# VectorE's order in an RWKV-7 mixer, state banks taken in two pairs, and a transpose step in two parts

## The chip, the core and the metric

The kernel runs on one core of one Trainium2 chip. The metric is the device time of one execution in microseconds (us), the median of several runs. A core has TensorE (matrix products and transposes, PE in the rows; its weight loads are PEld), VectorE (DVE), ScalarE (ACT), GpSimd (POOL) and SyncE (SP), which issues most of the DMAs. The engines run their own instruction streams and meet only at semaphores.

## The reference, cut to what matters

A trunk of two layers on x (512 tokens, 1024 features) in float32. Layer 0, the one that the change touches, runs two head groups behind one input projection:

```python
p = h @ ev_w_in                                   # 512 x (1792 + 1024)
y_a = rwkv7_time_mix(p[..., :1792], ...)          # 8 heads of 64
y_b = rglru_block(p[..., 1792:2304], p[..., 2304:], ...)
h = LayerNorm(alpha * h + concat(y_a, y_b) @ ev_w_out)
# inside rwkv7_time_mix
kk = kk / max(norm(kk), 1e-12)                    # norms per head
state = state * w_t + (state @ -kk_t) (kk_t * a_t)^T + v_t k_t^T
o = state @ r_t                                   # for each of 512 tokens
o = (o - mean) * rsqrt(var + 64e-5) * gn_g + gn_b # "group" norm per head
y_a = (o + bonus) * g
# inside rglru_block
h_t = a_t * h_{t-1} + u_t;  y_b = h * gelu(gb)
```

Then follow cross-attention to 256 memory tokens and an MLP of width 4096, and layer 1 (a conformer convolution and Mamba-2) with its own attention and MLP. All that is outside the mixer of layer 0 is left as it was.

## The kernel before

Every product of activations and weights is made of float32r parts: ScalarE rounds a tensor to its high part (`w_hi`, `act_hi`), VectorE subtracts to get the low part (`w_lo`, `act_lo`), and TensorE multiplies hi*hi, lo*hi and hi*lo. The weights come in chunks of 128x1024 through three raw slots `w_raw`; SP refills a raw slot once VectorE's `split` has made the chunk's low part (`w_split`).

The order of each engine is written out by hand, as Python code that issues one instruction after the other. No planner moves anything. What is planned is the eight PSUM banks: the table `TILES` deals them out in turn, and `take(name, i)` on TensorE waits until the bank's former owner has been read.

The mixer of layer 0 handles its 8 heads in two blocks `b` of 4 heads (two 128-feature halves `j` each) and its 512 tokens in 8 chunks of 64. In order of TensorE:

- the input projection, 22 tiles (`feature_major`, L778), with small steps of block b between: `norms(b)` sums squares of kk into one bank, VectorE's `norm_scales(b)` makes 1/norm (L2199, L2200, signal `r_norm`), and `norms_back(b)` (L932) spreads it over the features again. In block 1 VectorE's loop step i == 17 ran two convolutions (`convolution`, L2234 and L2154) before `norm_scales(1)`.
- `within_chunks(b)`: 8 banks `rprod` of products between tokens of a chunk (L958), which VectorE multiplies by masks (`masked_products(b)`, eight instructions of L2151 that read a bank and `m_two`). In the same banks follow 8 tiles `rtok`, transposes to token rows: six of L968, two of L970 that also take a mean away. Each waits for the mask product of its own bank. ScalarE copies the `rtok` tiles out. Then the two gate products of the LRU (`lru`, L1146), for which VectorE makes `convolution(0..3)`.
- a solve by doubling, five levels for both blocks (L997, L1012; VectorE's `level_y` and `level_z`), started from `first_level(b)` on VectorE (three kinds of L2151 and a transpose, L2304, signal `r_x0`); then `solved`, `even_output` and `transitions(b)` (L1042), whose sums VectorE adds (`added(b)`, signal `rat_out`).
- `scan()`: the 7 chunk states are gathered in the four `rst` banks, two chunks to a half bank; `states_from_tokens` (L1073) fills them in four steps m of two chunks, and m = 0, 1 write `rst` 0 and 1, m = 2, 3 write `rst` 2 and 3. The `rst` banks are those of `rat` of block 0. The outputs go to four `ro` banks (L1091, L1111).
- the output projection `out0` (L852) starts with the LRU half of the features (k = 0 to 3). Between k = 2 and k = 3 it calls `even_back` (L1138): 16 transposes of the normed RWKV outputs `oall`, 4 feature tiles jj times 4 token tiles m. `group_variance(m)` and `group_scale(m)` on VectorE make `oall[:, m]` (two signals `ro_out` each). VectorE's `lru_lo(k)` makes the low part of LRU feature tile k (signal `mix_lo`, k + 1); after that a chain of five instructions for each of the last four tiles gives `mix_lo` 5 to 8.

SP's queue around this place: chunk 5 of `out0`, the load of `h`, chunk 6 of `out0` (which waits for the low part of chunk 3, made by VectorE's `split(FIRST["out0"] + 1 + W_SLOTS)`), the load of `gb` (which waits for `mix_done`), chunk 7.

GpSimd works beside it: `r_times_k(1)` (L638, a product of two tensors), and memsets `clear` (L642), of which the first two wait for the 22nd projection tile.

Of the kernel before, what the change touches and what calls it, by code (L numbers as in the profile page):

```python
# [20 lines left out]
P = 128  # L21
# [3 lines left out]
NT = T // P  # L25
# [203 lines left out]
def build(nc, x_tok, x_feat, mem_feat, weights, vectors, lora, lru_w, ln_rows, out):  # L229
    with ExitStack() as ctx:  # L230
# [523 lines left out]
        def _(pe):  # L754
            def take(stg, i):

                if AFTER[stg, i]:
                    pe.wait_ge(*out_sem(*AFTER[stg, i]))
                return bank(stg, i)
# [287 lines left out]
            def scan():  # L1047
# [10 lines left out]

                def states_from_tokens():

                    for i in range(4):
                        take("rst", i)
                    for m in range(NT):
                        for jj in range(4):
                            b, j = divmod(jj, 2)
                            kt, v_ = operands(b)[5:7]
                            for n, (lhs, rhs) in enumerate([(kt, v_), (NBT[b], NBH[b])]):
                                for q in range(2):
                                    feat, ct = slice(RD * q, RD * q + RD), cols_(2 * m, q)
                                    for c in (2 * m, 2 * m + 1):  # L1070
                                        if c < NRC - 1:
                                            tok = rows_(c)
                                            last = pe.matmul(state(c)[feat, jj * RD:jj * RD + RD], lhs[tok, j, ct],  # L1073
                                                             rhs[tok, j, ct], start=(m % 2 == 0 and jj == 0 and n == 0),
                                                             stop=False, skip_group_check=True)
                    last.then_inc(S("rst_mm"), 1)
# [54 lines left out]

            def even_back():

                pe.wait_ge(S("ro_out"), 2 * NT)
                for jj in range(4):
                    o = take("rback", jj)
                    for m in range(NT):
                        last = pe.transpose(o[:, m * P:m * P + P], oall[:, m, jj * P:jj * P + P], ident[:])  # L1138
                    last.then_inc(S("mixer_mm"), 1)

            def lru():
# [968 lines left out]
        def _(dve):  # L2110
# [131 lines left out]
            for i in range(22):  # L2242
                stg, n = PLACE0[i]
                tile = ORDER0[i]
                split(i + W_SLOTS)
                if i < 14:

                    dve.wait_ge(S("r_in"), i + 1)
                    cur = p0[:, tile, PAD + 1:PW]
                    done(stt(cur, bank(stg, n)[:, 0:T - 1], V("mu", tile), cur, MUL, ADD), "in_out")  # L2250
                if i == 5:
                    scaled_keys(0)

                    dve.wait_ge(S("masks"), 1)
                    step(dve.tensor_scalar(small[:, 84:88], vec[:, VEC["ka"]:VEC["ka"] + 4], -1.0, 1.0, MUL, ADD))
                if i == 6:
                    running_decay(0)
                    keys(0)
                if i == 9:
                    norm_scales(0)  # L2260
                if i == 11:
                    normalised(0)
                    scaled_keys(1)
                if i == 12:
                    scale_operands(0, 0)
                if i == 13:
                    scale_operands(0, 1)
                if i == 14:
                    bonus(0)
                if i == 16:  # L2270
                    running_decay(1)
                    keys(1)
                if i == 17:
                    for j in range(2):
                        dve.wait_ge(S("in_out"), 15 + j)
                        convolution(j)
                if i == 17:
                    norm_scales(1)
                if i == 19:
                    normalised(1)  # L2280
                if i == 20:
                    scale_operands(1, 0)
                if i == 21:
                    scale_operands(1, 1)
# [23 lines left out]
            convolution(2)  # L2308
            first_level(0, 0, 1)
            bonus(1)  # L2310
            first_level(0, 1, 2)
            masked_products(1)
            dve.wait_ge(S("in_out"), 18)
            convolution(3)
            first_level(1, 0, 2)
# [56 lines left out]
            lru_scan(0)  # L2372
            lru_scan(1)
            added(0)
            lru_scan(2)
            added(1)
            lru_scan(3)

            def lru_lo(k):
# [24 lines left out]
            lru_lo(1)  # L2404
            for m in range(2):
                group_scale(m)
            lru_lo(2)
            for m in range(2, 4):
                group_variance(m)
            lru_lo(3)  # L2410
            for m in range(2, 4):
                group_scale(m)
            split(FIRST["out0"] + 1 + W_SLOTS)
            for jj in range(4):
                y_ = p0[:, jj, PAD:PW]
                dve.wait_ge(*made("rback", jj + 1))
# [8 lines left out]
                    done(tt(act_lo[:, 3 + jj], p0[:, jj - 1, PAD:PW], f(act_hi[:, 3 + jj]), SUB), "mix_lo")  # L2425
            dve.wait_ge(S("mix_hi"), 8)
            done(tt(act_lo[:, 7], p0[:, 3, PAD:PW], f(act_hi[:, 7]), SUB), "mix_lo")
            done(dve.tensor_copy(small[:, 255:256], small[:, 254:255]), "mix_done")

            n_rows = [0]  # L2430
# [558 lines left out]
```

## Time and profile before

| what | value |
|---|---|
| median of 3 runs (lowest, highest) | 1607.37 us (1607.27, 1607.51) |
| the profiled execution's own time | 1606.2 us |
| its span (first to last instruction) | 1604.1 us |
| mean granted TensorE clock | 0.996 of full speed |
| busy: PE, PEld, DVE, ACT, POOL | 97%, 81%, 73%, 53%, 12% |
| instructions | 24420 |

The span is 2.1 us shorter than the execution's own time, and the profiled execution was 1.2 us faster than the median of the unprofiled runs. The mixer of layer 0 takes the span's first 259 us. TensorE is busy nearly everywhere, so the short idle times in front of its instructions, and the stretches where its instructions follow each other more slowly than elsewhere, are the places to look at.

### The profile page before, as it was taken

How to read it: one execution, taken by the hardware profiler on the slowest of the kernel's cores; microseconds unless marked ns; L12 is line 12 of the kernel's file. 1: busy time of each engine (PE TensorE's matmuls, PEld its weight loads, DVE VectorE, ACT ScalarE, POOL GpSimd, SP SyncE). 2: the span in 40 equal slices, each digit the busy share in tenths (PEclk: the TensorE clock that was granted, in tenths of full speed). 3: DMA queues.
4: the chain of work that ended last, by engine and by line, in shares of the span. 5: the costliest groups of instructions: out<-in, count | busy, mean ns of one | idle time of the engine just before them, and what ended most of it. 6: DMA issues, size and time to landing. Idle time of an engine off the chain costs nothing.

```text
span 1604.1 us, 24420 instructions
## 1 busy us (share of the span) xinstructions
PE 1563.4 (97%) x9706; PEld 1300.4 (81%) x9706; DVE 1177.2 (73%) x1356; ACT 843.6 (53%) x1087; POOL 193.6 (12%) x189
## 2 busy tenths in 40 slices
PE   9999999999999999999899999999999999999996
PEld 8777887988878788888778877889888788888885
DVE  4569767664778868686979986786557788676768
ACT  4645644464355454554468866635552654545454
POOL 6111201001100000000016743200020000000001
PEclk9999999999999999999999999999999999999999
DMA  6222004442151505151032330344411605050501
GB/s 215 79 79 67 16 4 151 145 151 68 53 216 47 182 28 172 39 171 40 14 136 77 104 92 14 132 158 133 157 54 56 241 20 195 29 171 26 195 1 53
DMA packets 40784, 159.57 MB, mean 99 GB/s; under 512 B 4064, under 2 KB 4192, under 8 KB 39264
## 3 DMA queue, kind: packets, MB, share of 16 engines
q1 hardware_dynamic: 40384, 155.93, 28.8%
q10 hardware_dynamic: 288, 2.10, 0.3%
q8 instruction: 77, 1.26, 0.3%
q14 instruction: 35, 0.29, 0.1%
HBM read 153.81 MB, written 4.19 MB: 99 GB/s over the span
## 4 chain that ended last, share of the span: by engine, by line
PE 80%; DVE 11%; ACT 5%; issue 2%; POOL 1%; ACTq 0%; DVEq 0%; POOLq 0%
PE bank L778 40%; PE bank L1457 15%; PE bank L852 14%; DVE h L2151 2%; POOL cacc L702 1%; PE bank L1012 1%; PE bank L997 1%; DVE h L2154 1%; DVE mix L2151 1%; ACT cprod L1944 1%; DVE a_lo L2151 1%; DVE lnst L2651 1%; PE bank L1367 1%; ACT sconv L1958 1%; DVE w_lo L2138 1%
## 5 line engine op out<-in xcount | busy, mean ns | idle before, releaser
L778 PE MATMUL bank<-act_hi,w_hi 128*128 128x512 f32 x840 | 330.7, 394 | 2.1 <-DVE sconv L2154 1.8
L778 PE MATMUL bank<-act_lo,w_hi 128*128 128x512 f32 x840 | 326.5, 390 | 0.0
L2138 DVE TENSOR_TENSOR w_lo<-w_raw,w_hi 128x1024 fp32r<-128x1024 f32 x173 | 219.3, 1272 | 133.1 <-ACT w_hi L1574 130.0
L1574 ACT ACTIVATE w_hi<-w_raw 128x1024 fp32r<-128x1024 f32 x173 | 183.0, 1061 | 111.1 <-PE bank L852 78.3
L778 PE MATMUL bank<-act_hi,w_lo 128*128 128x512 f32 x840 | 212.0, 390 | 0.0
L778 PEld LDWEIGHTS bank<-act_hi,w_hi 128*128 128x128 f32 x840 | 158.0, 188 | 38.4 <-issue 2.6
L778 PEld LDWEIGHTS bank<-act_lo,w_hi 128*128 128x128 f32 x840 | 157.8, 188 | 34.0 <-issue 1.2
L778 PEld LDWEIGHTS bank<-act_hi,w_lo 128*128 128x128 f32 x840 | 157.7, 188 | 32.9 <-DVE w_lo L2138 0.3
L702 POOL TENSOR_TENSOR cacc<-cacc,cprod 128x512 f32<-128x512 f32 x52 | 72.3, 1391 | 456.0 <-ACT cprod L1944 453.5
L1898 ACT ACTIVATE bank<-bank 128x512 f32<-128x512 f32 x64 | 37.2, 582 | 166.7 <-PE bank L778 166.7
L852 PE MATMUL bank<-w_hi,act_hi 128*128 128x512 f32 x288 | 112.6, 391 | 1.5 <-DVE act_lo L2151 1.5
L852 PE MATMUL bank<-w_hi,act_lo 128*128 128x512 f32 x288 | 112.1, 389 | 0.0
L1889 ACT ACTIVATE a_hi<-a_raw 128x1024 fp32r<-128x1024 f32 x48 | 51.0, 1062 | 67.9 <-PE bank L1457 62.8
L778 PE MATMUL bank<-act_hi,x_hi 128*128 128x512 f32 x208 | 81.5, 392 | 0.7 <-ACT act_hi L1801 0.6
L778 PE MATMUL bank<-act_lo,x_hi 128*128 128x512 f32 x208 | 80.9, 390 | 0.2
L1457 PE MATMUL bank<-w_hi,a_lo 128*128 128x512 f32 x264 | 73.0, 391 | 3.0 <-DVE a_lo L2151 3.0
L852 PE MATMUL bank<-w_lo,act_hi 128*128 128x512 f32 x288 | 74.7, 389 | 0.0
L1457 PE MATMUL bank<-w_hi,a_hi 128*128 128x512 f32 x264 | 72.5, 389 | 0.0
L1457 PE MATMUL bank<-w_lo,a_hi 128*128 128x512 f32 x264 | 71.3, 389 | 0.0
L2151 DVE TENSOR_TENSOR h<-h,bank 128x512 f32<-128x512 f32 x96 | 65.7, 684 | 2.0
L2138 DVE TENSOR_TENSOR w_lo<-b_raw,w_hi 128x1024 fp32r<-128x1024 f32 x46 | 55.4, 1223 | 15.8 <-ACT w_hi L1574 15.1
L852 PEld LDWEIGHTS bank<-w_hi,act_hi 128*128 128x128 f32 x288 | 54.0, 188 | 12.9 <-issue 1.6
(374 smaller groups left out, 3039.9 us busy)
## 6 DMA issues: line engine op xcount, KB each, us to landing
w_raw<-weights SPq DMA_DIRECT2D x199, 512.0 KB, 3.5
b_raw<-weights SPq DMA_DIRECT2D x32, 1024.0 KB, 4.9
gb<-ln_rows SPq DMA_DIRECT2D x6, 1024.0 KB, 9.8
stage<-x_feat SPq DMA_DIRECT2D x4, 512.0 KB, 6.1
h<-x_tok SPq DMA_DIRECT2D x1, 2048.0 KB, 8.0
stage<-mem_feat ACTq DMA_DIRECT2D x2, 1024.0 KB, 7.4
spill<-h SPq DMA_DIRECT2D x1, 2048.0 KB, 9.0
h<-spill SPq DMA_DIRECT2D x1, 2048.0 KB, 7.7
```

The costliest lines, as they stand in the source:

```text
L702: pool.tensor_tensor(cacc2[:, j % 2], cacc2[:, j % 2], cprod[:, added % 2], ALU.add)\
L778: return pe.matmul(banks[i][:, 0:n], w(c0 + i)[:, k * P:k * P + P], x[:, k, 0:n], start=first, stop=last)
L852: return pe.matmul(o[t][:, 0:HALF], x[:, slot[k], t * P:t * P + P], w(c0 + k // 2)[:, kk * HALF:kk * HALF + HALF], start=first, stop=last)
L997: last = each(lambda c, q, tok, feat, cf, ct: pe.matmul(compact(o, j, c, q, n), M_[b][tok, j, ct], halves(NBH[b][tok, j, ct], n, True), st ...
L1012: last = each(lambda c, q, tok, feat, cf, ct: pe.matmul(compact(o, j, c, q, n), left[tok, j, ct], halves(right[tok, j, ct], n, v < 5), sta ...
L1367: ins = pe.transpose(o[:, t * P:t * P + P], h[:, t, k * P:k * P + P], ident[:])
L1457: return pe.matmul(o[t][:], a[:, slot, k, t * P:t * P + P], w(c0 + k // 2)[:, k % 2 * HALF:k % 2 * HALF + HALF], start=(after is None and ...
L1574: act.activation(hi_slot(c), raw_chunk(c), ACT.Copy).then_inc(S("w_hi_done"), 1)
L1889: done(act.activation(a_hi[:, n % 2], A_OPERAND[name], ACT.Copy), "x_hi")
L1898: step(act.activation(o[:], o[:], ACT.Relu))
L2138: dve.tensor_tensor(lo_slot(c), raw_chunk(c), f(hi_slot(c)), ALU.subtract).then_inc(S("w_split"), 1)
L2151: return dve.tensor_tensor(o, a, b_, op)
```

## The change

No instruction that computes is added or taken away. Seven things move:

1. `norm_scales(1)` runs ahead of `convolution(0)` and `convolution(1)`.
2. `masked_products(1)` runs ahead of `first_level(0, 1, 2)`, the second half of block 0's first level with its transpose.
3. `added(1)` runs ahead of `lru_scan(2)`.
4. TensorE takes `rst` 0 and 1 before m = 0 and `rst` 2 and 3 before m = 2, instead of all four at the start.
5. `even_back` makes the tiles jj = 0 and 1 side by side, token tile by token tile, and waits for 4, 6 and 8 signals `ro_out`; jj = 2 and 3 follow whole. Before, it waited for all 8 first.
6. `lru_lo(2)` goes between `group_variance(2)` and `group_variance(3)`, and `lru_lo(3)` behind the last `group_scale`.
7. the low part of chunk 3 of `out0` is made behind the chain of the last four feature tiles instead of ahead of it.

```diff
 def states_from_tokens():
-    for i in range(4):
-        take("rst", i)
     for m in range(NT):
+        if m % 2 == 0:
+            for q in range(2):
+                take("rst", m + q)
...
 def even_back():
-    pe.wait_ge(S("ro_out"), 2 * NT)
-    for jj in range(4):
+    def turned(o, jj, m):
+        return pe.transpose(o[:, m * P:m * P + P], oall[:, m, jj * P:jj * P + P], ident[:])
+    pe.wait_ge(S("ro_out"), 4)
+    first = [take("rback", jj) for jj in range(2)]
+    for m in range(NT):
+        if m >= 2:
+            pe.wait_ge(S("ro_out"), 2 * m + 2)
+        for jj in range(2):
+            last = turned(first[jj], jj, m)
+            if m == NT - 1:
+                last.then_inc(S("mixer_mm"), 1)
+    for jj in range(2, 4):
         o = take("rback", jj)
         for m in range(NT):
-            last = pe.transpose(...)
+            last = turned(o, jj, m)
         last.then_inc(S("mixer_mm"), 1)
...
                 if i == 17:
+                    norm_scales(1)
                     for j in range(2):
                         dve.wait_ge(S("in_out"), 15 + j)
                         convolution(j)
-                if i == 17:
-                    norm_scales(1)
...
             bonus(1)
+            masked_products(1)
             first_level(0, 1, 2)
-            masked_products(1)
...
             added(0)
+            added(1)
             lru_scan(2)
-            added(1)
             lru_scan(3)
...
             for m in range(2):
                 group_scale(m)
+            group_variance(2)
             lru_lo(2)
-            for m in range(2, 4):
-                group_variance(m)
-            lru_lo(3)
+            group_variance(3)
             for m in range(2, 4):
                 group_scale(m)
-            split(FIRST["out0"] + 1 + W_SLOTS)
+            lru_lo(3)
...
             done(tt(act_lo[:, 7], ...), "mix_lo")
+            split(FIRST["out0"] + 1 + W_SLOTS)
```

VectorE's stream where the masks of block 1 stand (`m_two` are the masks, `m_lev` and `eye_69` belong to the first level), before:

```order
81 L2151 TENSOR_TENSOR mix<-bank,mix 128x512 x2
82 L2151 TENSOR_TENSOR mix<-mix,m_lev 128x512
83 L2151 TENSOR_TENSOR mix<-mix,eye_69 128x512
84 L2304 STREAM_TRANSPOSE mix<-mix 128x1024
85 L2151 TENSOR_TENSOR mix<-bank,m_two 128x2x4x64 x8
86 L2234 TENSOR_SCALAR lc<-mix,vec 128x512
```

The same place after:

```order
81 L2163 TENSOR_TENSOR mix<-bank,mix 128x512 x2
82 L2163 TENSOR_TENSOR mix<-bank,m_two 128x2x4x64 x8
83 L2163 TENSOR_TENSOR mix<-mix,m_lev 128x512
84 L2163 TENSOR_TENSOR mix<-mix,eye_69 128x512
85 L2315 STREAM_TRANSPOSE mix<-mix 128x1024
86 L2246 TENSOR_SCALAR lc<-mix,vec 128x512
```

The eight mask products move ahead of three instructions of the first level; the convolution behind them keeps its place.

VectorE's stream at the end of the mixer (`oall` is written by `group_scale`, `act_lo` by `lru_lo`), before:

```order
144 L2151 TENSOR_TENSOR oall<-bank,small 128x4x64 x2
145 L2151 TENSOR_TENSOR act_lo<-mix,act_hi 128x512
146 L2389 TENSOR_REDUCE small<-mix 128x8 x2
147 L2151 TENSOR_TENSOR act_lo<-mix,act_hi 128x512
148 L2395 RECIPROCAL small<-small 128x8
149 L2151 TENSOR_TENSOR oall<-bank,small 128x4x64 x2
150 L2395 RECIPROCAL small<-small 128x8
151 L2151 TENSOR_TENSOR oall<-bank,small 128x4x64 x2
152 L2138 TENSOR_TENSOR w_lo<-w_raw,w_hi 128x1024
```

And after:

```order
143 L2163 TENSOR_TENSOR oall<-bank,small 128x4x64 x2
144 L2400 TENSOR_REDUCE small<-mix 128x8
145 L2163 TENSOR_TENSOR act_lo<-mix,act_hi 128x512
146 L2400 TENSOR_REDUCE small<-mix 128x8
147 L2406 RECIPROCAL small<-small 128x8
148 L2163 TENSOR_TENSOR oall<-bank,small 128x4x64 x2
149 L2406 RECIPROCAL small<-small 128x8
150 L2163 TENSOR_TENSOR oall<-bank,small 128x4x64 x2
151 L2163 TENSOR_TENSOR act_lo<-mix,act_hi 128x512
152 L2166 SCALAR_TENSOR_TENSOR mix<-bank,vec,mix 128x512
```

One `act_lo` product leaves the stretch ahead of the last `oall`, and the `w_lo` product no longer stands ahead of the chain for the last tiles.

## Rows read from the trace of the kernel before

**Rows 1.** The page, section 1: busy us, share of the span, instructions

```profile
PE 1563.4 (97%) x9706; PEld 1300.4 (81%) x9706; DVE 1177.2 (73%) x1356; ACT 843.6 (53%) x1087; POOL 193.6 (12%) x189
```

**Rows 2.** What TensorE waited for, 100 to 262 us: total, times, longest

```profile
PE bank L932 <- DVE small L2200: 1.3, 1, 1.3
PE bank L1073 <- issue: 1.1, 1, 1.1
...
PE bank L1073 <- DVE mix L2151: 0.5, 1, 0.5
```

**Rows 3.** Timeline of TensorE: start, us, instruction [idle before <-releaser]

```profile
160.49 4.28 PE L968 MATMUL bank<-ident,mix 128*128 128x128 f32 x24 [0.75 <-DVE mix L2151]
164.84 2.05 PE L970 MATMUL bank<-center,mix 128*128 128x128 f32 x16
166.72 7.03 PE L1146 MATMUL bank<-lc,lru_sb 128*128 128x512 f32 x16
```

**Rows 4.** Timeline of VectorE, 110 to 146 us, with one row from 52.80

```profile
52.80 4.78 DVE L2191 TENSOR_SCALAR mix<-mix,vec,small 128x512 f32<-128x512 f32 x2
...
121.76 2.63 DVE L2234 TENSOR_SCALAR lc<-mix,vec 128x512 f32<-128x512 f32 x1
...
126.78 0.55 DVE L2234 TENSOR_SCALAR lc<-mix,vec 128x512 f32<-128x512 f32 x1
...
129.94 0.25 DVE L2200 RECIPROCAL small<-small 128x16 f32<-128x16 f32 x1
...
142.64 0.18 DVE L2221 COPY dend<-mix 128x16 f32<-128x16 f32 x1
...
145.37 5.76 DVE L2151 TENSOR_TENSOR mix<-bank,m_two 128x512 f32<-128x512 f32 x8
```

**Rows 5.** Timeline of VectorE around the masks of block 1

```profile
157.01 0.69 DVE L2151 TENSOR_TENSOR mix<-mix,m_lev 128x512 f32<-128x512 f32 x1
...
159.74 5.77 DVE L2151 TENSOR_TENSOR mix<-bank,m_two 128x512 f32<-128x512 f32 x8
```

**Rows 6.** The chain that ended last, 310 to 330 us: start, us, what

```profile
318.76 2.62 PE bank L1367 x24
```

**Rows 7.** Timeline of ScalarE: the first gate of the LRU

```profile
172.17 0.69 ACT L1698 ACTIVATE mix<-bank,vec 128x512 f32<-128x512 f32 x1
```

**Rows 8.** Timeline of GpSimd

```profile
52.85 2.40 POOL L630 TENSOR_TENSOR mix<-mix 128x1024 f32<-128x1024 f32 x1 [22.62 <-DVE dend L2184]
55.21 2.08 POOL L632 TENSOR_TENSOR mix<-dend,mix 128x1024 f32<-128x1024 f32 x1
...
120.66 3.44 POOL L638 TENSOR_TENSOR mix<-mix 128x1024 f32<-128x1024 f32 x1 [1.62 <-DVE mix L2151]
...
143.38 1.85 POOL L642 MEMSET hall<- 128x1024 f32 x2 [19.28 <-PE bank L778]
```

**Rows 9.** Timeline of VectorE: the sums of the transitions

```profile
225.19 2.85 DVE L2151 TENSOR_TENSOR mix<-mix,bank 128x512 f32<-128x512 f32 x4 [4.15 <-PE bank L1042]
```

**Rows 10.** Timeline of TensorE at the transposes back, and in out0

```profile
257.45 1.97 PE L1138 MATMUL bank<-ident,oall 128*128 128x128 f32 x16 [1.75 <-DVE oall L2151]
259.17 0.47 PE L852 MATMUL bank<-w_hi,act_hi 128*128 128x512 f32 x1
...
264.73 0.40 PE L852 MATMUL bank<-w_hi,act_hi 128*128 128x512 f32 x1
```

**Rows 11.** Timeline of VectorE at the end of the mixer

```profile
254.40 0.69 DVE L2151 TENSOR_TENSOR act_lo<-mix,act_hi 128x512 fp32r<-128x512 f32 x1
...
263.83 0.69 DVE L2151 TENSOR_TENSOR act_lo<-mix,act_hi 128x512 fp32r<-128x512 f32 x1
```

**Rows 12.** Timeline of SP's queue, 225 to 310 us

```profile
258.68 0.33 SPq L524 DMA_DIRECT2D w_raw<-weights  x1
267.77 0.33 SPq L545 DMA_DIRECT2D gb<-ln_rows  x1
```

**Rows 13.** The page, section 6: DMA issues, KB each, median us to landing

```profile
h<-x_tok SPq DMA_DIRECT2D x1, 2048.0 KB, 8.0
```

More of the change, by code:

```diff
@@ L1132, in even_back @@
             def even_back():
-                pe.wait_ge(S("ro_out"), 2 * NT)
-                for jj in range(4):
+                def turned(o, jj, m):
[10 more added lines that the diff above has]
+                for jj in range(2, 4):
                     o = take("rback", jj)
                     for m in range(NT):
-                        last = pe.transpose(o[:, m * P:m * P + P], oall[:, m, jj * P:jj * P + P], ident[:])
+                        last = turned(o, jj, m)
                     last.then_inc(S("mixer_mm"), 1)
```

## The prediction, made before the changed kernel was run

> **What bounds the kernel now.** I began with the page's busy lines: TensorE is busy for 97% of the span, the next engine for 73% [rows 1], and its mean granted clock is 0.996 of full speed. So a change elsewhere pays only where TensorE stands still or is slowed, and the sum of such places is small. The second view was TensorE's waits in the mixer of layer 0. Three lines belong to places that the change touches: 1.3 us before L932 (the norms of block 1), 0.5 us before L1073 (the sums of the transitions), and 1.1 us inside L1073 for which no releaser is seen [rows 2]. Two more stand in the timeline: 0.75 us before L968 and 1.75 us before L1138 [rows 3, 10]. That is 5.4 us in all. The third view, the timeline, was needed for what a wait list hides: an engine that waits a little before each of many short groups. L968 of block 1 takes 4.28 us for 24 transposes [rows 3], where 24 such transposes elsewhere take 2.62 us [rows 6]. There TensorE follows VectorE's mask products, one bank at a time.
>
> **Norms of block 1: worth nothing.** The reciprocal ends at 130.19 and L932 starts 1.3 us late [rows 2, 4]. With the norms ahead of the convolutions it is ready some 5 us sooner, and TensorE arrives at the products of block 0 about 1.3 us earlier. But what follows there are tiles in banks that VectorE frees by its eight masks of block 0, and these start at 145.37, directly behind VectorE's own queue [rows 4]; that queue holds the same instructions as before. So the 1.3 us turn into a longer wait a few microseconds later. I take 0. The floor is a small loss, as follows.
>
> **What moving them costs on VectorE.** A one-source VectorE instruction on 512 columns takes 0.55 us [rows 4], but 2.63 us at 121.76, where GpSimd's L638 runs until 124.10 [rows 4, 8]: it had to wait for GpSimd. After the change the small maximum (128x16) stands in that place. I let it wait in the same way; then the convolution behind it starts clean, and the queue is about 0.2 us late, of which a wait of 0.17 us for ScalarE's next chunk, before 134.07, takes most. I charge 0.07. The second meeting is new: GpSimd's two memsets of 1.85 us follow the 22nd projection tile, so they move from 143.38 to about 142.07, and VectorE's copy of 0.18 us at 142.64 now falls beside them [rows 4, 8]. No row shows a copy beside a memset. Bounds: nothing, if they pass each other; 1.28 us, if the copy waits for both memsets (142.07 + 1.85 + 0.18 against 142.82). The nearest row is the pair of L2191, 4.78 us beside L630 and L632 [rows 4, 8]: each waited for one GpSimd instruction and got in before the next. By that the copy waits for one memset, until 143.0, and ends 0.35 us late. I take 0.35, and 0.42 with the 0.07. All of it reaches TensorE, since the masks of block 0 set its pace.
>
> The trace shows a VectorE instruction stretched from 0.55 to 2.63 us beside a GpSimd one. The Trainium skill (SBUF — State Buffer, "Who interferes with whom") has the rule: copies and tensor_scalar that use both port pairs and any GpSimd instruction exclude each other, and the later one blocks fully. It counts the memset in, though that only writes. The trace agrees for tensor products on GpSimd; for a memset no run here shows it yet. By the rule the price lies at 0.35 or above, never 0.
>
> **Masks of block 1: 2.5 us less that 0.42.** Before, VectorE spends 157.01 to 159.74 on the rest of the first level and then frees banks at 5.77 / 8 = 0.72 us each [rows 5]. TensorE was ready at 160.49 - 0.75 = 159.74 [rows 3]. After, the masks start at 157.01; their products exist, because TensorE makes them in four pairs of 0.93 us, the last done by 159.74, the first by 157.0. The last bank is free at 157.01 + 8 * 0.72 = 162.77. TensorE starts the tiles at 159.74, runs six of L968 in 2.62 [rows 6] and two of L970 in 166.72 - 164.84 = 1.88 [rows 3]; it comes to the last bank at 163.3, after it is free. L1146 thus starts at 159.74 + 2.62 + 1.88 = 164.24 and not 166.72: 2.48 us. Less 0.42 this is 2.06.
>
> What is late next? VectorE makes the fourth convolution in the same place, behind 159.74 + 5.77 = 165.5 [rows 5]; it takes 2.9 us (from 126.78 to the norms [rows 4]) and ends at 168.4, or 168.9 with the delay; the last pair of L1146 (7.03 us for four pairs [rows 3]) needs it 5.3 us after its start, at 169.9. ScalarE's first gate starts at 172.17 [rows 7] and ends at 172.86, 0.8 us before TensorE is through with L1146 at 173.7 and needs its bank. ScalarE's copies of the tiles follow TensorE's, so the gate comes about 2.2 us earlier too, with 0.6 us to spare. The first level of block 0 is now done last, at 165.9, and is needed after L1146, near 173.5. Each cover is enough, if some only just. The doubling levels that follow are paced by TensorE on every instruction, so the shift is kept.
>
> **Sums of the transitions: 0.5 us.** Four `added` products take 2.85 us from 225.19, 0.71 each [rows 9]. TensorE waited 0.5 us for the fourth; for the first two `rst` banks the second is enough, at 226.6, a microsecond before TensorE comes. The other two come free at 228.05, when TensorE is 0.4 us into its first 64 products and still has 1.7 to go. The stall of 1.1 us in L1073 [rows 2] has no semaphore behind it, no data is missing, and I read it as a supply of instructions that short products outrun. The products keep their places in the stream, so it should stay; bounds 0 (it grows by the 0.5) and 1.6 (it goes). `added(1)` comes earlier by 2.7 us, for a wait that was already covered: 0. The scan of the LRU is later by the same, and its readers come 10 us afterwards: 0.
>
> **The end of the mixer: 1.3 us.** One `act_lo` of 0.69 us (0.72 with the gap) [rows 11] leaves the stretch before the last `oall`, so this is ready at 256.7 instead of 257.43. By then TensorE, which reaches the place at 255.7, has done 6 of 16 transposes. The whole 16 took 259.17 - 257.45 = 1.72 us to the next start [rows 10], so 10 take 1.08: L852 goes on at 257.8, 1.36 earlier. It needs `lru_lo(3)`, ready at 257.4. The chain behind starts 1.15 us earlier, since the `w_lo` product of 1.23 is out of its way but `lru_lo(3)` in front; TensorE is 1.36 earlier. For feature tile 5 the low part was ready at 264.52 and needed at 264.73 [rows 10, 11], so the 0.21 to spare just vanish; I charge 0.05. The moved `w_lo` is ready at 267.6 and needed at 267.9. `lru_lo(2)` is 0.7 later, at 253.65, needed at 253.73. Sum 1.3; bounds 0.7 (if the thin covers each fail by a little) and 1.5.
>
> **Sum.** 0 + 2.06 + 0.5 + 1.3 = 3.9 us of a span of 1604.1. Nothing behind the mixer has a clock of its own: weights are fetched when slots come free. So the execution of 1606.2 us becomes 1602.3, and the median, which stood 1.2 above it, 1607.37 - 3.9 = 1603.5.
>
> **The rivals.**
>
> *Short gain, 1605.0.* A cover fails: the copy waits for both memsets (1.28, not 0.35), and one of the thin spots costs 0.5. Then 3.9 - 0.93 - 0.5 = 2.5 us. For it: slacks of 0.03 to 0.6 us in five places. Against: each is worked out from contiguous rows. Both memsets ahead of the copy, and nothing else, give 1603.5 + 0.9 = 1604.4. Chance 0.27 for all of this. The rule of the Trainium skill named above is on its side.
>
> *All waits go, 1602.2.* Copy and memsets pass each other (+0.42) and the stall in L1073 disappears (+1.1), 5.4 us minus what the thin covers keep: 5.2. For it: moving a start changes when instructions are fetched. Against: the 16 KB pieces are fetched as they are used up. Chance 0.08.
>
> *No change, 1607.* The mask shift is lost again because TensorE stands before the gate products or the solve, on ScalarE or on `r_x0`. It would need those to be 2 us later than worked out. Chance 0.04.
>
> *Slower than before, 1608.5.* The chunk 6 load of `out0` waits for the moved low part: it goes out at 267.6 instead of 258.68, together with `gb` [rows 12], the memory tokens and chunk 7, 3 MB at once. TensorE wants its high part at 283, so every microsecond that it lands after 282 is lost. From 286 on the gain is eaten, and a landing at 287, 19 us after its issue, makes 1608.5. Against: the 2 MB of `h` land in 8.0 us [rows 13], and 3 MB at that rate take 12 and are in by 280. Chance 0.04.
>
> **How the numbers follow.** My forecast has the remaining 0.57. What a measurement of this kernel can tell from no change is about 0.2%, 3.2 us, that is below 1604.2 or above 1610.6. The forecast is mostly on the faster side, the second rival wholly, the first about one part in five; a slice of the forecast (0.04) lies above 1604.2. The last rival passes 0.2% in half of its part. Faster 0.66, same 0.32, slower 0.02. Range: 1602.2 from the second rival, 1606.0 from the first with a second thin spot failing.
>
> **What would show it.** In the changed profile: no wait before L932; the masks of block 0 starting at or up to 1.3 us after 145.37, with the copy of `dend` longer than 0.18 us if it waited; L968 of block 1 at about 2.7 us for 24; the gate products starting about 2.1 us earlier; no DVE wait before the state products, and still 1.1 us of no releaser; the transposes back in two pieces with a short wait between, and TensorE 3.9 us ahead by the time `out0` goes on. I am wrong if the gate products start less than 1.5 us earlier, or if a new wait stands between them and the end of `out0`.

## The result: 24.8 us slower, and the profile after

The changed kernel takes 1632.12 us, the median of 5 runs (1631.02 to 1632.53), against 1607.37 of the kernel before. The ratio is 1.0156, 95% interval [1.0145, 1.0167]. The prediction was 1603.5 and the chance given to slower was 0.02: it was wrong, in sign and size. In the profile the span is 1628.9 us, the execution 1631.02.

The page, section 1 (answers to [rows 1]) and the line of section 2 that gives TensorE's granted clock in 40 slices of 40.7 us, in tenths of full speed:

```profile
PE 1589.7 (98%) x9706; PEld 1328.5 (82%) x9706; DVE 1178.4 (72%) x1356; ACT 843.3 (52%) x1087; POOL 194.1 (12%) x189
...
PEclk9999759999999999999999999999999999999998
```

TensorE has the same 9706 instructions and is busy 26.3 us longer, its weight loads 28.1; the three other engines are within 1.2 us of before. So nothing was added; instructions became slower. The fifth and sixth digits (163 to 244 us) say where. Three stretches of the kernel after: us, then each engine's busy us, then the granted clock, the share of the DMA engines, GB/s:

```profile
174.00:183.00 9.00, 8.04 (x274) 7.92 (x271) 4.29 (x6) 7.00 (x10) 3.48 (x3) 0.99 0.19 62
183.00:241.00 58.00, 58.00 (x1065) 58.00 (x1064) 27.00 (x34) 14.35 (x16) 11.02 (x9) 0.50 0.01 2
241.00:262.00 21.00, 19.16 (x541) 16.58 (x539) 14.88 (x20) 11.93 (x19) 0.00 (x0) 1.00 0.01 3
```

The middle one in the kernel before:

```profile
183.00:241.00 58.00, 56.39 (x1785) 53.58 (x1783) 42.31 (x53) 26.91 (x36) 11.01 (x9) 1.00 0.02 4
```

For 58 us TensorE had the lower of its two levels, 1.2 GHz, and did 1065 products where the kernel before did 1785 at 2.4 GHz. TensorE's waits, 100 to 262 us (the places of [rows 2]): total, times, longest:

```profile
PE bank L1074 <- issue: 1.7, 1, 1.7
PE bank L968 <- DVE mix L2163: 1.6, 1, 1.6
PE bank L1012 <- issue: 1.0, 1, 1.0
```

The waits at L932, at L1073 for VectorE and at L1138 have all gone, as forecast. One is new: 1.0 us inside L1012, the doubling levels of the mixer, for no semaphore. (That the engines meet only at semaphores, as said above, is too narrow: this loss came without one, and so did the longer copy on VectorE below.) The timeline of TensorE from the tiles of block 1 on (answers to [rows 3]; L1158 is the old L1146):

```profile
161.11 2.84 PE L968 MATMUL bank<-ident,mix 128*128 128x128 f32 x24
163.79 2.04 PE L970 MATMUL bank<-center,mix 128*128 128x128 f32 x16
165.66 7.03 PE L1158 MATMUL bank<-lc,lru_sb 128*128 128x512 f32 x16
...
174.54 3.87 PE L997 MATMUL bank<-mix 64*64 64x32 f32 x128
178.25 1.91 PE L1012 MATMUL bank<-hall,mix 64*64 64x32 f32 x58
181.12 2.52 PE L1012 MATMUL bank<-hall,mix 64*64 64x32 f32 x70 [0.96 <-issue]
...
190.18 7.11 PE L1012 MATMUL bank<-mix 64*64 64x32 f32 x128
...
237.97 8.66 PE L1027 MATMUL bank<-mix 64*64 64x128 f32 x128
246.55 3.70 PE L1130 MATMUL bank<-mix,lora_sb 128*128 128x512 f32 x8
```

And the same levels in the kernel before:

```profile
175.60 3.87 PE L997 MATMUL bank<-mix 64*64 64x32 f32 x128
179.31 3.90 PE L1012 MATMUL bank<-hall,mix 64*64 64x32 f32 x128
...
213.16 7.23 PE L1027 MATMUL bank<-mix 64*64 64x128 f32 x128
```

To compare two profiles I measure from L920, the last group ahead of the change: it starts at 116.05 us before and at 115.95 after, and in the experiments up to 1.0 later for no reason that lies in the edits. So counted, L997 starts 0.96 us earlier than before (58.59 against 59.55). Up to 178 us the change gains. Then TensorE stands still for 0.96 us in the middle of a group. The record of the granted clock falls at 182.88 us, 1.8 us after TensorE went on, and rises at 240.9, inside L1027. In between a group of 128 products of 64x32 takes 7.11 us, where it took 3.90. The sum: from the first L997 to L1027 it is 63.4 us, before 37.6 (213.16 - 175.60), so 25.9 lost; L1027 and L1130, 12.2 instead of 10.8, lose 1.4. Less the 0.96 this makes 26.3, and L1042 indeed starts 26.3 us later (134.23 from L920, before 107.91). The back half then returns 0.8, so that `out0` goes on 25.5 us later; the medians differ by 24.8.

What was TensorE waiting for? Traffic of the DMA engines from 172 to 184 us, GB/s in 40 slices of 0.3 us, first the kernel before:

```profile
GB/s 0 0 0 0 0 0 82 0 0 27 164 205 273 396 396 273 14 0 0 0 55 0 0 0 0 0 0 0 0 0 0 0 55 0 0 0 0 0 0 0
```

and the kernel after, with its queues in that stretch (packets, MB, share):

```profile
GB/s 0 0 0 0 82 0 0 0 0 0 0 0 0 0 0 123 177 109 273 423 355 259 27 55 0 0 0 0 0 0 0 0 0 0 55 0 0 0 0 0
...
q1 hardware_dynamic: 144, 0.52, 13.4%
q8 instruction: 3, 0.05, 1.6%
```

The broad hump is one weight load of 512 KB; the single slices of 55 are fetches of TensorE's instructions, 16 KB each, on q8. That q8 is TensorE's is read from its pace: in the levels it starts a fetch every 3.75 to 3.84 us before, where a group of 128 products takes 3.73, and every 6.1 to 7.3 us after, where a group takes 6.83 at 1.2 GHz. By the packets' own times, the load ran from 174.93 to 177.02 before, and the next fetch started at 178.04. After, the load ran from 176.58 to 178.91, and the fetch started at 178.91, the moment the load had ended. The load is that of chunk 5 of `out0`, released by the `w_lo` product that VectorE makes last before the levels. TensorE was 0.96 us earlier, and this product 1.77 later (58.39 from L920, before 56.62), because a copy and a wait for `rprod` (below) put VectorE's queue back. Two things that had passed each other by a microsecond met.

VectorE at the places of [rows 4] and [rows 5], and GpSimd at that of [rows 8]:

```profile
121.66 2.36 DVE L2211 TENSOR_SCALAR small<-small 128x16 f32<-128x16 f32 x1
...
142.54 1.23 DVE L2233 COPY dend<-mix 128x16 f32<-128x16 f32 x1
...
146.32 5.77 DVE L2163 TENSOR_TENSOR mix<-bank,m_two 128x512 f32<-128x512 f32 x8
...
158.68 5.77 DVE L2163 TENSOR_TENSOR mix<-bank,m_two 128x512 f32<-128x512 f32 x8 [0.74 <-PE bank L958]
...
174.34 1.23 DVE L2150 TENSOR_TENSOR w_lo<-w_raw,w_hi 128x1024 fp32r<-128x1024 f32 x1
```

```profile
141.90 1.84 POOL L642 MEMSET hall<- 128x1024 f32 x2 [17.91 <-PE bank L778]
```

The small maximum waited for L638 as forecast. The copy waited for both memsets: it took 1.23 us where it had taken 0.18, so it ended 1.05 late and not 0.35. The masks of block 0 start 1.05 us later from L920 (30.37, before 29.32), and those of block 1 wait 0.74 us for their products.

### The profile page after: what moved, and what is told of

It is laid out like the page before. It is cut to its first block, busy times and chain, and to the rows that moved or that the text cites. A ratio compares the mean times of both kernels' runs of the same rounds, so it can differ in the third digit from the quotient of the medians.

```text
span 1628.9 us, 24420 instructions
## 1 busy us (share of the span) xinstructions
PE 1589.7 (98%) x9706; PEld 1328.5 (82%) x9706; DVE 1178.4 (72%) x1356; ACT 843.3 (52%) x1087; POOL 194.1 (12%) x189
## 4 chain that ended last, share of the span: by engine, by line
PE 80%; DVE 11%; ACT 5%; issue 3%; POOL 1%; ACTq 0%; DVEq 0%; POOLq 0%
PE bank L778 39%; PE bank L1469 14%; PE bank L852 14%; PE bank L1012 2%; PE bank L997 2%; DVE h L2163 2%; POOL cacc L702 1%; DVE h L2166 1%; ACT cprod L1956 1%; DVE w_lo L2150 1%; DVE a_lo L2163 1%; DVE mix L2163 1%; PE bank L1379 1%; DVE lnst L2662 1%; ACT sconv L1970 1%
```

## The experiments

**1. The norms alone** (edit 1 of the change put into the kernel before), and **2. the masks alone** (edit 2):

```diff
                 if i == 17:
+                    norm_scales(1)
                     for j in range(2):
```
```diff
+            masked_products(1)
             first_level(0, 1, 2)
-            masked_products(1)
```

> The kernel before with one edit of the seven: norm_scales(1) ahead of the two convolutions. Theory A (a weight load in front of TensorE's instruction fetch starves it, and the half clock follows from that stall): VectorE's copy of dend waits for both memsets, the masks of block 0 start 0.95 us later (146.3), the load of the next weight chunk goes out about 0.95 us later (176 to 178) and is over before the fetch that is due about 179. No stall in L1012, at most one stretch of 3.4 us at half clock near 148; 1608 to 1609 us. Theory B (the low clock comes from the longer wait before L968 at 147, which primes the later fall): the clock falls for some 58 us here too, 1630 us.

> The kernel before with one edit: masked_products(1) ahead of first_level(0, 1, 2). Theory A: TensorE comes to the doubling levels 2.3 us earlier, while VectorE's last low weight part, and so the chunk load behind it, stay where they were (load 175 to 177.3). The instruction fetch is due at 175.7, waits behind the load until 177.3, TensorE stalls 0.5 to 0.7 us in the first levels and the clock falls to half until out0: 1628 to 1632 us. Theory B (the wait before L968 of block 0): no such wait grows here, no fall, 1605 us. Theory C (the fall comes from TensorE being earlier against whatever watches its activity, with no part of the load): a fall without a stall of no releaser before it.

Norms alone: 1607.84 us against 1607.06, ratio 1.0003 [0.9994, 1.0012]. The wait at L932 goes, but the copy of `dend` takes 1.22 us, and L997 starts 60.61 us after L920: 1.06 later than before. The edit by itself is a small loss, in the trace, and none that the times can tell. Masks alone: 1633.54, ratio 1.0162 [1.0148, 1.0176]. So this one swap brings the whole loss. Yet up to the levels it gains all that was forecast: L997 starts 57.05 us after L920, 2.50 earlier. Its timeline of TensorE:

```profile
174.05 3.87 PE L997 MATMUL bank<-mix 64*64 64x32 f32 x128
177.76 1.91 PE L1012 MATMUL bank<-hall,mix 64*64 64x32 f32 x58
180.63 3.06 PE L1012 MATMUL bank<-hall,mix 64*64 64x32 f32 x70 [0.96 <-issue]
```

The stall stands behind the same 58th product and is as long: a place in the instruction stream, not a datum. The `w_lo` product is only 0.23 us later here; it is TensorE that came to meet the load. The load ran to 178.34, and the fetch started at 178.34. The clock was at 1.2 GHz from 181.74 to 243.18.

The 3.4 us at 1.2 GHz that the kernel after has at 148.7, ahead of the loss, are not there in experiment 2, so the loss does not need them.

**3. The load earlier in the kernel after**, and **4. the load later in the kernel before.** One moves `split(FIRST["out0"] + W_SLOTS)` ahead of `convolution(3)`, the other behind the first `level_y`:

```diff
             first_level(0, 1, 2)
+            split(FIRST["out0"] + W_SLOTS)
             dve.wait_ge(S("in_out"), 18)
             convolution(3)
             first_level(1, 0, 2)
-            split(FIRST["out0"] + W_SLOTS)
```
```diff
             first_level(1, 0, 2)
-            split(FIRST["out0"] + W_SLOTS)
...
                     level_y(b, v)
+                    if v == 1 and b == 0:
+                        split(FIRST["out0"] + W_SLOTS)
```

> The changed kernel with one more edit: the low part of chunk 2 of out0 is made before convolution(3) and not behind first_level(1), so that the chunk load runs 169.4 to 171.6, where no instruction fetch is due. The fourth convolution ends 1.2 us later and TensorE waits about 0.5 us for it. Theory A: no stall in L1012, the clock stays up through the levels, 1604 to 1605.5 us. Theories B and C: the clock falls as before, 1630 us.

> The kernel before with one edit: the low part of chunk 2 of out0 is made behind VectorE's first level_y product and not behind first_level(1), so that the chunk load runs from 180.7 to 183. TensorE's own order and VectorE's results for it move by 0.1 us at most. Theory A: the instruction fetch that was at 181.8 starts only at 183, TensorE stalls and the clock falls to half for some 50 us: 1627 to 1632 us. The lateness of the fetch is 1.2 us where 1.9 us made a stall of 0.96, so the stall may be as short as 0.2 us and then be too small for a fall. Theories B and C: 1607.5 us, no fall.

The first: 1604.91, ratio 0.9985 [0.9976, 0.9994]. The load ran from 169.49 to 171.64, no stall in the levels, and the 25 us are gone, with all seven edits in place. The second: 1607.30, ratio 1.0002 [0.9992, 1.0012]. Its load (180.72 to 182.81) held a fetch up until 182.81, but TensorE stood only 0.26 us there, and the profile shows no fall. One of its ten runs took 1631.63, with a mean granted clock of 0.979 where the nine others had 0.995 to 0.997. So a collision by itself is not enough; the runs suggest that it has to hold TensorE up for longer.

Where no load is near, this fetch starts 1.87 to 2.64 us after the first L997 (experiments 3, 4, 7 and 8).

**5. A standstill without a load.** Eleven copies of 128x1 on VectorE between the first two `level_y` of the kernel before:

```diff
                     level_y(b, v)
+                    if v == 1 and b == 0:
+                        for _ in range(11):
+                            step(dve.tensor_copy(small[:, 255:256], small[:, 254:255]))
```

> The kernel before with eleven tiny copies (128x1, some 2.0 us together) put into VectorE's queue between its first two level_y products; no DMA is moved. TensorE's second group of the first level_z (L1012) then waits about 1.1 us for VectorE at 181. Theory A (any standstill of about a microsecond at this place lets the clock fall, whatever its cause): the clock falls to half for some 50 to 60 us, 1631 us. Rival D (the fall needs the starved instruction stream or the load itself): only the wait is paid, 1608.2 to 1609.5 us.

1607.23, ratio 1.0 [0.9991, 1.001]. This settled nothing about a standstill, since TensorE did not stand still. It does show that such copies on VectorE cost nothing by themselves:

```profile
179.52 4.02 PE L1012 MATMUL bank<-hall,mix 64*64 64x32 f32 x128
183.37 3.90 PE L997 MATMUL bank<-mix 64*64 64x32 f32 x128
```

I had overlooked that the group's second 64 products come 2 us after its first, and need the delayed block only then. Experiments 10 and 11 repeat it with enough copies.

**6. The back half of the change alone** (edits 3 to 7, with 1 and 2 undone):

> The changed kernel without the first two edits, that is, the kernel before with edits 3 to 7 (added(1) earlier, rst banks in pairs, the transposes back in two parts, lru_lo and the low part of chunk 3 moved). Nothing moves before 225 us, so the load and the fetches of the levels stay where they were in the kernel before. Theory A: no fall of the clock; 0.5 us at the sums of the transitions and 1.3 us at the transposes, 1605.3 us against 1607.1. If these edits had their part in the fall: 1630 us.

1605.17 against 1606.84, ratio 0.9987 [0.9979, 0.9996]: 1.7 us gained, 1.8 forecast for these terms.

**7. The load held back**: the kernel after, and SP waits with this one load for the eighth `rt` tile, which brings it to 221 us, behind the levels. **8.** The same, and GpSimd's first two memsets wait until VectorE has made the two products behind its copy of `dend`:

```diff
                     sp.wait_ge(S("w_split"), RAW_PREV[c] + 1)
+                if c == FIRST["out0"] + 5:
+                    sp.wait_ge(*made("rt", 8))
                 sp.dma_start(w_raw[:, RAW[c]], weights[SOURCE[c]])...
```
```diff
             pool.wait_ge(S("chunk_done"), 22)
+            pool.wait_ge(S("r_ops"), 2)
             clear(yt_(0, 1), 0)
```

> The changed kernel, with every compute engine's order untouched; only SP waits for the end of solved() (made('rt', 8), about 220 us) before it issues the load of chunk 5 of out0. Theory A: that load no longer stands before the instruction fetch due at 177, no stall in L1012, no fall over the levels; 1604.0 to 1605.0 us. Theories B and C (the fall comes from TensorE's or VectorE's new timing): 1630 us.

> The kernel of the run before, and GpSimd also waits for r_ops(1) before its first two memsets, so that VectorE's copy of dend has no memset beside it. Theory A: the copy takes 0.18 us again, the masks of block 0 start at 145.4 and not 146.3, TensorE is 0.95 us earlier from there, and the stretch of 3.4 us at half clock at 148.7, which follows a wait of 1.6 us, goes or not: 1602.8 to 1604.0 us. If the copy was not held by the memsets: no difference from the run before.

Held: 1603.34 against 1606.84, ratio 0.9980 [0.9971, 0.9989]. Held and memset: 1602.35, ratio 0.9969 [0.9957, 0.9981], the fastest version, ahead of both kernels. The two intervals overlap, so that the second wait is worth 1.0 us rests on the medians and on the trace. VectorE, GpSimd and TensorE of the last:

```profile
143.62 0.18 DVE L2236 COPY dend<-mix 128x16 f32<-128x16 f32 x1
143.83 2.48 DVE L2166 TENSOR_TENSOR mix<-mix 128x1024 f32<-128x1024 f32 x2
146.35 5.77 DVE L2166 TENSOR_TENSOR mix<-bank,m_two 128x512 f32<-128x512 f32 x8
...
158.22 5.77 DVE L2166 TENSOR_TENSOR mix<-bank,m_two 128x512 f32<-128x512 f32 x8 [0.26 <-PE bank L961]
```

```profile
146.44 1.84 POOL L644 MEMSET hall<- 128x1024 f32 x2 [21.38 <-DVE mix L2166]
```

```profile
174.08 3.87 PE L1000 MATMUL bank<-mix 64*64 64x32 f32 x128
...
222.59 3.72 PE L1045 MATMUL bank<-mix 64*64 64x128 f32 x128
226.14 2.62 PE L1077 MATMUL bank<-mix 64*64 64x64 f32 x166
229.72 1.44 PE L1077 MATMUL bank<-mix 64*64 64x64 f32 x55 [0.96 <-issue]
...
253.61 0.81 PE L1139 MATMUL bank<-ident,oall 128*128 128x128 f32 x6
254.63 1.31 PE L1139 MATMUL bank<-ident,oall 128*128 128x128 f32 x10 [0.20 <-DVE oall L2166]
255.69 0.48 PE L855 MATMUL bank<-w_hi,act_hi 128*128 128x512 f32 x1
```

The copy is at 0.18 us again. From L920 (117.03 here) TensorE is ahead of the kernel before by 2.50 us at the first level, 2.35 at L1042 and 4.46 when `out0` goes on (138.66, before 143.12).

**9. The load alone moved.** The kernel before, with twelve copies of 128x1 ahead of that `split`, in 3.8 us in which VectorE was idle:

```diff
             first_level(1, 0, 2)
+            for _ in range(12):
+                step(dve.tensor_copy(small[:, 255:256], small[:, 254:255]))
             split(FIRST["out0"] + W_SLOTS)
```

**10 and 11. The standstill again**, with 17 and 25 copies in the place of experiment 5.

> The kernel before with twelve copies of 128x1 put ahead of the last weight split of the mixer on VectorE, where VectorE was idle for 3.8 us: nothing but the release of the 512 KB load moves, by 12 x 0.186 = 2.2 us, from 174.9 to about 177.1-179.4. TensorE's next instruction fetch, at 178.04 before (and 177.5 where no load stands ahead of it), then waits until the load has ended. Theory C (the load in front of the fetch is the whole cause): TensorE stands about 1 us in L1012, the clock falls to 1.2 GHz at about 183 and stays there to about 241, time 1632 to 1634 in every run. Rival D (it also needs the earlier start of the doublings that masked products first give): no fall, 1607 to 1608.

> As the stall of eleven copies, in which TensorE turned out not to stand still at all (the second half of its products needed the block only 2.0 us after the first): now seventeen copies, so the second masked block ends at about 182.5 and TensorE waits about 1.1 us in the middle of L1012's group, for VectorE, with its instructions at hand and no load or fetch displaced. Theory A (a standstill of about 1 us among the short products is enough, whatever its cause): clock at 1.2 GHz for about 58 us, 1632 to 1634. Theory B (only the late instruction stream, with what follows it, does it): clock stays, 1607 + at most 1.1 = 1607.5 to 1608.3.

> The same with twenty-five copies: TensorE waits about 2.6 us in the middle of L1012's group. Theory A: fall, 1633 to 1635, whatever the seventeen copies do. Theory B: no fall, 1609 to 1610.

The load alone: of ten runs five took 1607.4 to 1609.2 us and five 1633.4 to 1634.9, against 1607.14. The mean granted clock was 0.995 to 0.997 in the first five and 0.977 to 0.979 in the others. The ratio over the first five is 1.0005 [0.9993, 1.0017]: where the clock held, the edit cost nothing. The profiled run is one of the long ones:

```profile
179.55 1.91 PE L1012 MATMUL bank<-hall,mix 64*64 64x32 f32 x58
181.86 2.83 PE L1012 MATMUL bank<-hall,mix 64*64 64x32 f32 x70 [0.40 <-issue]
184.40 7.12 PE L997 MATMUL bank<-mix 64*64 64x32 f32 x128
```

Its load ran from 177.40 to 179.68, and the fetch started at 179.48, 3.64 us after the first L997.

With 17 copies: 1635.02 us, 4 runs, all above 1633, ratio 1.017 [1.0153, 1.0187]. With 25: 1638.55, ratio 1.0195 [1.018, 1.021]. TensorE with 17:

```profile
179.51 2.03 PE L1012 MATMUL bank<-hall,mix 64*64 64x32 f32 x64
182.61 3.63 PE L1012 MATMUL bank<-hall,mix 64*64 64x32 f32 x64 [1.07 <-DVE hall L2151]
...
233.83 7.02 PE L1012 MATMUL bank<-mix,hall 64*64 64x32 f32 x128
240.66 8.74 PE L1027 MATMUL bank<-mix 64*64 64x128 f32 x128
```

Here the load (175.12 to 177.92) and the fetch (178.25) are in nobody's way, TensorE has its instructions and waits 1.07 us for VectorE, and the clock falls all the same, from 182.44 to 243.88. Of experiment 10's theories A holds and B does not: at this place it matters that TensorE stands still, not why. Of experiment 9's theories neither holds as written. C is right that the load alone can do it, but it said every run, and it was half of them; D, that there would be no fall, is wrong. The stall of 0.40 us is shorter than in the kernel after; that this is why only half the runs fell is likely and not shown, since none of the short runs has a profile.

Several times lay outside the ranges that I had put down for the theory that held: 1607.84 us in experiment 1 (1608 to 1609), 1633.54 in 2 (1628 to 1632), 1603.34 in 7 (1604 to 1605), 1602.35 in 8 (1602.8 to 1604), 1635.02 in 10 (1632 to 1634) and 1638.55 in 11 (1633 to 1635); in 4 the fall that was expected came in one run of ten. The rivals, 20 us and more away, are told apart all the same in 1, 2, 3, 6, 7, 10 and 11.

Taken together: the start of the fetch after the first L997, TensorE's standstill in the levels (both from the profile), and the runs:

| version | fetch after | stall | runs at the long time |
|---|---|---|---|
| before | 2.44 us | none | none of 73 |
| back half (6) | 3.00 | 0.27, elsewhere | none of 11 |
| load later, before (4) | 1.87, the next one held up | 0.26 | 1 of 10, not the profiled |
| load alone (9) | 3.64 | 0.40 | 5 of 10 |
| masks alone (2) | 4.29 | 0.96 | 4 of 4 |
| after | 4.37 | 0.96 | 5 of 5 |
| 17 copies (10) | 2.45 | 1.07, on VectorE | 4 of 4 |
| 25 copies (11) | 2.46 | 2.57, on VectorE | 4 of 4 |

The table holds for the levels alone. The stall inside L1073, among products of 64x64, was 0.96 to 1.70 us long in all thirteen profiles, and in none did the clock fall there. So a microsecond of standstill brings the clock down among the 64x32 products of the levels, and not among short products everywhere.

## Why the prediction was wrong

**The step that failed** is in the part on the masks: "The doubling levels that follow are paced by TensorE on every instruction, so the shift is kept". In the sum this is no term at all for the stretch from the first L997 to L1027, 37.6 us long, which became 63.4. I had looked for data and banks that could be late in the levels, and there are none. I left out two resources. One was TensorE's own instruction stream: I had named the 1.1 us in L1073 as a supply of instructions, so the trace had shown me that short products run that supply dry, and I did not ask what traffic it shares a path with. The other was the granted clock: the 0.996 was taken as given. Neither was among the rivals, nor was the DMA that the moved instructions release: I followed every instruction of the swap except the last `w_lo` product, which starts the load of chunk 5. The two rivals nearest to it had something else in mind: a late landing of chunk 6 at the end of the mixer, and a wait before the gate products or the solve for data of ScalarE or `r_x0`.

**The rest of the forecast: the total near, the terms less so.** With the one load out of the way, experiment 7, the same seven edits measure 1603.34 us where 1603.5 was forecast: 3.5 us gained against the 1606.84 of the kernel before beside it, where 3.9 was forecast. That it comes so near is in part luck. Its profiled execution took 1605.68, 2.3 above its median, and in it TensorE is, from L920, ahead by 1.00 us at the first L997 (2.06 forecast), behind by 0.18 at L1042, and ahead by 1.10 when `out0` goes on (3.9 forecast). What the faster executions did otherwise, no profile shows. By term:

- Norms: 0 forecast, and TensorE's 1.3 us did turn into a longer wait before L968. This wait, now 1.58 us, had a price that I did not see: in the profiles of after and of experiments 3 and 7 the clock was at 1.2 GHz for 3.4 us behind it (148.7 to 152.2 in the first), and L968 took 5.00 us instead of the 4.28 of experiment 1, where the wait was the same and the clock held. That is 0.48 us until L940.
- Port delay: 0.42 forecast, 1.06 measured (1). The copy waited for both memsets, the upper bound of that term. The row I had chosen, L2191, which got in between two GpSimd instructions, was the wrong neighbour; why the copy did not get in between the two memsets, no run here shows. The rule of the Trainium skill (SBUF — State Buffer, "Who interferes with whom"), that a VectorE copy in the mode with two ports and a GpSimd instruction block each other fully, with no exception for GpSimd instructions that only write, now agrees with the trace: 0.18 us became 1.23, and was 0.18 again when the memsets moved.
- Masks: 2.48 us forecast, 2.50 measured in experiment 2. In the kernel after, 2.50 - 1.06 - 0.48 = 0.96, which is what L997 gained, where 2.06 was forecast.
- Transitions: 0.5 forecast. The wait for VectorE is gone (no such row after). The issue wait at its side, 1.1 before, is 1.70 after, 1.47 in experiment 7 and 0.96 in 8: it moves both ways. In 7 and 8 it stays inside the bounds given; in the kernel after it grew by 0.6, a tenth more than the lower bound had room for. I read this as the phase of the fetches; no run tests it.
- End of the mixer: 1.3 forecast; from the end of L1073's stall to `out0` going on it took 27.21 us before, 26.56 after, 26.29 in experiment 7, 25.97 in 8 and 25.76 in 6: 0.65 to 1.45 less. TensorE waits 0.2 us between the two pieces in each. In the profiles of experiments 1, 2, 4, 5, 9 and 10, which have the old back half, it took 27.2 to 27.8 us, so a single profile tells such a term to some 0.6 us.
- Transitions and end together: 1.8 forecast; the edits alone bring 1.7 by the medians (6) and 2.1 in their profile (L1042 to `out0`, 33.12 us instead of 35.21, where the six profiles just named have 35.5 to 35.9).

**The two signs of being wrong** both showed: "wrong if the gate products start less than 1.5 us earlier" (165.66 against 166.72), "or if a new wait stands between them and the end of `out0`" (0.96 us in L1012).

**What stays open.** Why TensorE does not return to 2.4 GHz while the short products run, though they kept 2.4 GHz before, is not shown; the runs show only that in each of the five profiles with a fall over the levels it came back inside L1027, the first group behind them. Why a standstill brings the clock down in the levels and not in L1073 is not shown either. In the levels, a stall of 0.26 us did nothing in its profile and 0.96 or more came with a fall in every run; in between there is only the 0.40 of experiment 9. And that the fetch queues behind the load's packets is read from times that coincide (178.91 and 178.91, 178.34 and 178.34) and from experiments that moved the load; the queues themselves are not seen. In experiment 9 the fetch started 0.20 us before the load's last packet ended, so it does not wait for the whole load, perhaps only for the part on one of the sixteen DMA engines.

## What to carry to other kernels

In a stretch of short TensorE instructions, treat instruction fetches as transfers with due times and keep large loads out of their way, by moving the load and not the fetch. A standstill there can cost far more than its length: in these levels 0.96 to 1.07 us, whatever the cause, made the kernel 25 to 28 us longer through the clock. When an edit moves two things towards each other, list every DMA that the moved instructions release, and read the distance to its neighbours in the trace, before adding up the waits that go. And a kernel that is slower with the same instructions should be asked first for its granted clock.

## What the runs showed of the hardware

- A standstill of TensorE of 0.40 to 2.57 us among products of 64x32 brought, in five profiles (from 0.96 us up in every run, at 0.40 in half of them), the granted clock from 2.4 to 1.2 GHz at most 2 us past its end, and it stayed there for 58 to 61 us, at 7.0 to 7.1 us for 128 products instead of 3.9. In these five the clock came back inside L1027. Stalls of 0.96 to 1.70 us among products of 64x64 (L1073, thirteen profiles) left it up. After a wait of 1.58 us ahead of L968 (transposes of 128x128) it was down for 3.4 us in three profiles; after the 1.57 us of experiment 1 it was not.
- A fetch of 16 KB started when a 512 KB load had ended (178.91, 178.34, and 182.81 in experiment 4), or 0.20 us before its last packet (179.48, experiment 9). The Trainium skill (Runtime: NRT & Kernel Launch, "Instruction fetch mechanics") says that instructions come in blocks of 16 KiB through a DMA queue of the engine's own, and that the fetch is hidden because instructions are issued more slowly than they come. The size agrees with this trace (16 KB each); that it is hidden does not: it cost 0.96 us in L1012 and, by my reading, 1.1 to 1.7 in L1073.
- The slack of that supply can be read off the table: the fetch may start 3.0 us after the first L997 and nothing is lost, and the stalls put the limit at 3.64 - 0.40 = 3.2 to 4.37 - 0.96 = 3.4 us, an estimate from three profiles. Short gaps of 0.2 to 0.3 us without a releaser stand in the levels of experiments 6 and 7 too, where no load is near; they differ from profile to profile. That they are why runs of one kernel differ by 2 us is a guess.
